# State-space scan with running sums loaded as rows, one input product for the context, and the last expert pair combined from SBUF

## What is computed

```python
a = (dt * A)                                   # per token and head, negative
a_cs = cumsum(a, in the chunk)                 # running sums
decay_to_end = exp(a_cs[..., -1:] - a_cs)
states = einsum('bclgn,bcgrl,bclgrp->bcgrpn', Bc, decay_to_end, xs * dt)
...
seg = a_cs[..., :, None] - a_cs[..., None, :]
Lm = exp(where(lower, seg, -inf))
cb = einsum('bclgn,bcsgn->bcgls', Cc, Bc)
y_diag = einsum('bcgls,bcgrls,bcsgrp->bclgrp', cb, Lm, x)
y_off = einsum('bclgn,bcgrpn,bcgrl->bclgrp', Cc, h_prev, exp(a_cs))
```

## Time and profile before

| | us |
|---|---|
| three runs | 3544.15, 3545.57, 3545.67 |
| median | 3545.57 |
| the profiled execution | 3550.36 |
| its span, first to last instruction | 3548.5 |

### The profile page before, as it was taken

One profiled execution on the slowest core, in us unless ns is written; L12 is line 12 of the kernel. 1 busy time (PEld: TensorE's weight loads), 2 busy tenths in 40 slices (PEclk: granted clock), 3 DMA queues, 4 the chain that ended last, 5 costly groups with the idle time before them and its releaser, 6 DMA issues. The chain is left out here.

```text
span 3548.5 us, 38000 instructions
## 1 busy us (share of the span) xinstructions
PE 3138.4 (88%) x15866; PEld 1657.4 (47%) x15866; DVE 1070.3 (30%) x2066; ACT 560.3 (16%) x1183; POOL 287.7 (8%) x270
## 2 busy tenths in 40 slices
PE   6997789998999999898999999997996789997984
PEld 5444644564554444653344434433545763544331
DVE  2233712554573301410111011103146453522112
ACT  2001510211452200100000000002012212301111
POOL 0003000002751000000000000000001200001101
PEclk9998999998899999899999999999998999997997
DMA  7721021110001222469999999997310012053996
GB/s 268 257 76 48 1 75 36 48 36 0 25 1 48 94 71 71 190 279 428 427 428 427 427 428 426 428 428 290 129 36 2 3 69 91 13 201 132 409 425 274
DMA packets 132081, 669.35 MB, mean 189 GB/s; under 512 B 17578, under 2 KB 45645, under 8 KB 98889
## 3 DMA queue, kind: packets, MB, share of 16 engines
q1 hardware_dynamic: 115385, 630.24, 44.0%
q10 hardware_dynamic: 11488, 28.31, 2.1%
q0 software_dynamic: 5040, 8.40, 0.7%
HBM read 672.15 MB, written 14.69 MB: 194 GB/s over the span
## 5 line engine op out<-in xcount | busy, mean ns | idle before, releaser
L2013 PE MATMUL ec_wide<-ec_ring,ec_xg 128*64 128x512 f32 x2048 | 459.8, 603 | 18.0 <-issue 13.8
L2013 PEld LDWEIGHTS ec_wide<-ec_ring,ec_xg 128*64 128x64 f32 x2048 | 147.9, 139 | 309.5 <-issue 305.4
L2047 PE MATMUL ec_acc<-ec_ring,ec_hidT 128*64 128x512 f32 x1024 | 233.6, 611 | 29.2 <-DMA ec_ring<-in_w_exp_down 28.4
L2172 DVE TENSOR_SCALAR ec_xg<-ec_piece,ordered 128x128 f32<-128x128 f32 x64 | 21.9, 404 | 570.8 <-PE ec_piece L2061 570.8
L2047 PEld LDWEIGHTS ec_acc<-ec_ring,ec_hidT 128*64 128x64 f32 x1024 | 81.9, 141 | 177.9 <-issue 177.8
L2061 PEld LDWEIGHTS ec_piece<-ec_sel,x 128*128 128x128 f32 x512 | 122.9, 336 | 8.6 <-issue 5.7
L2061 PE MATMUL ec_piece<-ec_sel,x 128*128 128x128 f32 x512 | 124.4, 405 | 2.8 <-DVE ec_sel L2154 2.8
L3700 PE MATMUL hm_gu<-hm_ring,hm_xg 128*64 128x512 f32 x432 | 115.7, 604 | 8.0 <-DMA hm_ring<-in_moe_w_gu 5.4
L2750 POOL TENSOR_TENSOR solve_T<-const_rw,solve_T 128x512 f32<-128x512 f32 x8 | 10.1, 1266 | 1311.7 <-DVE solve_T L2788 1311.7
L2136 ACT ACTIVATE ec_hidT<-ec_acc 128x512 f32<-128x512 f32 x32 | 17.4, 594 | 518.9 <-PE ec_acc L2036 518.9
L1151 PE MATMUL conv_main<-hT,conv_early 128*128 128x512 f32 x192 | 86.2, 604 | 2.9 <-DVE bcT L1233 2.9
(11 more groups left out here) (638 smaller groups left out, 5009.4 us busy)
## 6 DMA issues: line engine op xcount, KB each, us to landing
ec_ring<-in_w_exp_gate SPq DMA_DIRECT2D x64, 2048.0 KB, 17.7
ec_ring<-in_w_exp_up SPq DMA_DIRECT2D x64, 2048.0 KB, 27.0
ec_ring<-in_w_exp_down SPq DMA_DIRECT2D x64, 2048.0 KB, 19.5
hm_ring<-in_moe_w_gu SPq DMA_DIRECT2D x27, 2048.0 KB, 25.5
hm_ring<-in_moe_w_down SPq DMA_DIRECT2D x11, 2048.0 KB, 29.2
ahead_qkv<-in_w_in SPq DMA_DIRECT2D x10, 2048.0 KB, 9.7
hm_ring_late<-in_moe_w_down SPq DMA_DIRECT2D x5, 2048.0 KB, 25.2
u2T<-in_moe_w_gu SPq DMA_DIRECT2D x5, 2048.0 KB, 23.6
```

The source lines that it names most:

```text
L2013: last = pe.matmul(wide[half(e), b, :], xg[:, u % 2, j, half(e)], w[e][:, a, b * 512:(b + 1) * 512], start=(j == 0), stop=(j == KD - 1))
L2047: last = pe.matmul(acc[half(e), h, :], hidT[:, f, half(e)], w[e][:, r, h * 512:(h + 1) * 512], start=(f == 0), stop=(f == FT - 1))
```

## The change

In `steps_and_conv`: TensorE makes 8 more products behind the sums (running sums with the heads as rows), ScalarE copies them to `cumT`, copies the running sums with the tokens as rows into `a`, and stores `cumT` to DRAM (`cum_rows`); VectorE multiplies the decay to the end by `dt` once for all units. In `ssd_scan`: SP loads, per main unit, 1024 running sums into all 128 partitions (`crow`, 512 KB, 4 buffers, two of them in `hcT`); ScalarE forms max(0, own sum - row) in place and then its exponential with a minus; seg and seg_in are gone; `cb` has two buffers; xde is made from x directly, and context units have no xd. In `fine_experts`: the output of the last pair isn't stored; TensorE multiplies it by a one-hot matrix that carries the shares, VectorE adds the product, and the 8 loads no longer wait for the last pair.

```diff
@@ steps_and_conv, tensor, scalar, vector @@
+                for d, (bank, name) in enumerate(((prod, "upto"), (side[:, 1, :], "from"))):
+                    for t in range(LT):
+                        last = pe.matmul(bank[0:32, t * P:(t + 1) * P], a[:, t, d * 32:(d + 1) * 32], k.const(name), start=True, stop=True)
+                    last.then_inc(rows_summed, 1)
...
+            for d, bank in enumerate((prod, side[:, 1, :])):
+                act.wait_ge(rows_summed, d + 1)
+                act.activation(cumT[:, d, :], bank[0:32, :], ACT.Copy).then_inc(rows_taken, 1)
+            act.activation(a[:, :, :].rearrange("p t h -> p (t h)"), sums[0][:, 0:2 * N_SEG * 32], ACT.Copy).then_inc(exp_out, 1)
...
+            act.dma_start(cum_rows.rearrange("d t h l -> h d t l"), cumT.rearrange("h d (t l) -> h d t l", l=P)).then_inc(rows_stored, 16)
...
+                if i == R + 2:
+                    dve.wait_ge(decays_ready, 1)
+                    for d in range(2):
+                        m = slice(d * N_SEG, (d + 1) * N_SEG)
+                        dve.tensor_tensor(dec[:, m, 32:64], dt[:, :, d * 32:(d + 1) * 32], dec[:, m, 32:64], ALU.mult).then_inc(ended, 1)
@@ ssd_scan, sync @@
+            for m, n in enumerate(mains):
+                _, d, c, g = units[n]
+                unit = (d * LT + c) * SSD_G + g
+                if m >= CROWS:
+                    sp.wait_ge(exped, m - CROWS + 1)
+                sp.dma_start(crow[m % CROWS].rearrange("p h l -> p (h l)"), groups[unit:unit + 1, :].to_broadcast([P, HG * P])
+                             ).then_inc(crow_loaded[m % CROWS], 16)
+                if m == CROWS - 1:
+                    sp.wait_ge(inputs_ready, mains[0])
+                    then(sp)
@@ gpsimd @@
-                ins = pool.tensor_tensor(xd[:, n % 2].rearrange("p (h e) -> p h e", h=HG), x,
-                                         spread(dt[:, tile(units[n]), hs:hs + HG], 64), ALU.mult)
-                if n >= kept:
-                    ins.then_inc(inputs_ready, 1)
-                    return
-                link(ins)
...
+                if main:
+                    ins = pool.tensor_tensor(xd[:, n % 2].rearrange("p (h e) -> p h e", h=HG), x,
+                                             spread(dt[:, tile(units[n]), hs:hs + HG], 64), ALU.mult)
+                if n < kept:
+                    ins = pool.tensor_tensor(xde[:, n % 2].rearrange("p (h e) -> p h e", h=HG), x,
+                                             spread(dec[:, d * N_SEG + tile(units[n]), 32 + g * HG:32 + (g + 1) * HG], 64), ALU.mult)
+                ins.then_inc(inputs_ready, 1)
@@ tensor @@
-                for h in range(2):
-                    pe.matmul(seg[:, h, :], k.const("after" if d == 0 else "before"),
-                              seg_in[:, m % 2, 4 * h:4 * h + 4].rearrange("p h l -> p (h l)"), start=True, stop=True)
-                pe.matmul(cb[:, 0:P], bT[:, g, c * P:(c + 1) * P], cT[:, g, c * P:(c + 1) * P], start=True,
-                          stop=True).then_inc(seg_ready, 1)
+                if m >= 2:
+                    pe.wait_ge(masked, m - 1)
+                pe.matmul(cb[:, m % 2, 0:P], bT[:, g, c * P:(c + 1) * P], cT[:, g, c * P:(c + 1) * P], start=True,
+                          stop=True).then_inc(cb_ready, 1)
@@ scalar @@
+                for h in range(HG):
+                    row = crow[m % CROWS][:, h, :]
+                    ins = act.activation(row, row, ACT.Relu, scale=-1.0, bias=cum[:, d * N_SEG + c, g * HG + h:g * HG + h + 1])
+                ins.then_inc(falls_ready, 1)
...
+                act.activation(lx[:, m % 2], crow[m % CROWS], ACT.Exp, scale=-1.0).then_inc(exped, 1)
@@ fine_experts, gpsimd, tensor, scalar, vector @@
-            for b in range(2):
-                pool.wait_ge(y_stored[b], 16 * HM_PAIRS // 2)
-            pool.wait_ge(down_done, HM_PAIRS)
+            pool.wait_ge(y_stored[0], 16 * (HM_PAIRS // 2))
+            pool.wait_ge(y_stored[1], 16 * (HM_PAIRS // 2 - 1))
+            pool.wait_ge(down_done, HM_PAIRS - 1)
...
+                    for t in range(LT):
+                        last = pe.transpose(list_[:, t * P:(t + 1) * P], sel[:, u % 2, t, :], k.const("ident"))
+                    last.then_inc(weights_turned, 1)
...
+                for h in range(2):
+                    last = pe.matmul(combined[t % 2][:, h, :], sel[:, HM_PAIRS % 2, t, :], y[:, (HM_PAIRS - 1) % 2, h * 512:(h + 1) * 512],
+                                     start=True, stop=True)
+                last.then_inc(last_product, 1)
...
+                if u == HM_PAIRS - 1:
+                    act.wait_ge(weights_turned, 1)
+                    act.activation(sel[:, HM_PAIRS % 2, :, :].rearrange("p t n -> p (t n)"), list_[:, :], ACT.Copy).then_inc(weights_ready, 1)
...
+                    dve.scalar_tensor_tensor(out[:, t, :], back[:, 2 * t + i, :], earlier[:, i, t:t + 1], out[:, t, :], ALU.mult, ALU.add).then_inc(added, 1)
+                dve.wait_ge(last_product, t + 1)
+                dve.wait_ge(added, 3 * t + 2)
+                dve.tensor_tensor(out[:, t, :], out[:, t, :], combined[t % 2][:, :, :].rearrange("p b n -> p (b n)"), ALU.add).then_inc(added, 1)
```

More of the change, by code:

```diff
@@ L1076, in free, with steps_and_conv @@
         self.early.close()
-def steps_and_conv(k, hT, hcT, steps_in, weights, vec, taps, work, dt, a, dec, bcT, b_rows, bc_rows, xs, xsc):
+def steps_and_conv(k, hT, hcT, steps_in, weights, vec, taps, work, dt, a, decays, bcT, b_rows, bc_rows, xs, xsc):
     nc = k.nc
@@ L1796, in first_mixer @@
                     dec = tile(s1, "dec", [P, 2 * N_SEG, 96])
+                    cum_rows = nc.dram_tensor("ssd_cum_rows", [2, LT, SSD_H, P], F32, kind="Internal").ap()
                     bcT = tile(s1, "bcT", [P, 2 * SSD_G, L])
@@ L3782, in gathered_tokens, with last_weights @@
                                   scale_cols.unsqueeze(2).to_broadcast([P, KD, P]), ALU.mult).then_inc(xg_ready, 1)
+            def last_weights():
+                u = HM_PAIRS - 1
+                for e in range(2):
+                    link(dve.scalar_tensor_tensor(weight[:, e], first[:, :, :], float((2 * u + e) * SLOTS - 1), here[:, :, :], ALU.is_equal, ALU.mult))
+                    link(dve.tensor_tensor(weight[:, e, 0, :], weight[:, e, 0, :], weight[:, e, 1, :], ALU.add))
+                    dve.tensor_tensor(sel[:, u % 2, :, half(e)], sel[:, u % 2, :, half(e)],
+                                      weight[:, e, 0, :].unsqueeze(2).to_broadcast([P, LT, SLOTS]), ALU.mult).then_inc(weighted, 1)
+                link(dve.scalar_tensor_tensor(earlier[:, :, :], first[:, :, :], float(last_rows) - 1.5, here[:, :, :], ALU.is_lt, ALU.mult))
             one_hots(0)
@@ L3802, in _ @@
                     gathered_tokens(u + 1)
-            for n in range(BACK):
-                t, i = n // 2, n % 2
-                dve.wait_ge(fetched[n], 16)
-                if i:
-                    dve.wait_ge(added, n)
-                dve.scalar_tensor_tensor(out[:, t, :], back[:, n, :], here[:, i, t:t + 1], out[:, t, :], ALU.mult, ALU.add).then_inc(added, 1)
+                if u + 3 == HM_PAIRS:
+                    last_weights()
+            for t in range(LT):
+                for i in range(2):
+                    dve.wait_ge(fetched[2 * t + i], 16)
+                    if i:
+                        dve.wait_ge(added, 3 * t + i)
+                    dve.scalar_tensor_tensor(out[:, t, :], back[:, 2 * t + i, :], earlier[:, i, t:t + 1], out[:, t, :], ALU.mult, ALU.add).then_inc(added, 1)
+                dve.wait_ge(last_product, t + 1)
+                dve.wait_ge(added, 3 * t + 2)
+                dve.tensor_tensor(out[:, t, :], out[:, t, :], combined[t % 2][:, :, :].rearrange("p b n -> p (b n)"), ALU.add).then_inc(added, 1)
             link(dve.tensor_scalar(rank[:, :, :], rank[:, :, :], -float(SLOTS), None, ALU.add))
```

99 lines of the change are left out of this document (54 added, 45 removed).

## The result

| | before | changed |
|---|---|---|
| median, 20 runs each (us) | 3548.99 (3544.15 to 3554.21) | 3554.36 (3550.30 to 3558.81) |
| ratio, 95% interval | | 1.0014, 1.0008 to 1.0020 |
| span of the profiled execution (us) | 3548.5 | 3551.6 |
| TensorE, VectorE, ScalarE, GpSimd busy (us) | 3138.4, 1070.3, 560.3, 287.7 | 3132.7, 1082.4, 563.6, 264.3 |

The changed kernel is 0.14% slower, some 5 us (2.8 to 7.1), which is less than the 0.2% named as "no change"; with 20 runs each the interval leaves 1 out, so the small loss is real. Two large products a unit are gone from TensorE, yet its busy time fell by only 6 us: the work that is left there runs at a lower clock.

What follows compares the result with a forecast made beforehand. TensorE was taken to bound convolution and the first sixteen main units, GpSimd and VectorE next. Terms 1.8 - 2.6 - 0.5 - 3.4 + 1.7 - 5.0 - 2.1 + 12.8 = +2.7 on 3545.57 gave 3548.3 us; range 3531 to 3563.

Steps and rivals of the forecast that it cites:

- way into the main units: Between context and main units: a seg is lost, but cb, st, yo, yd run serially at low clock; -0.5 (-1.5 to +0.5).
- first sixteen, clock held: First sixteen main units at 2.4 GHz: unit falls from 5.45 to 5.24 us, -3.4 in all.
- last eight, clock held: Last eight main units at 2.4 GHz: unit falls from 5.93 to 5.1 us, -5.0 in all.
- clock falls, last sixteen and first sixteen: Main units: pauses without seg cause eight falls of 1.6 us, +12.8 (+5 to +21); none in the first sixteen.
- experts: End of experts: loads start 5.65 us earlier, eight adds, four PSUM adds and one 0.9 wait follow; -2.1 (-4 to +0.5).
- Only one runs at a time, and the one that came first goes first: Scan: any GpSimd instruction, mix and the late add into y exclude each other; early unit 5.24 us.
- the port isn't the next bound: Rival, main units: VectorE gets its operands first, early units come down to 4.5 us; 3522.9 in all, chance 0.08.
- some units reach 6.35. I take 6.2: Third eight main units: queueing gives 5.84, a delaying decay 6.35; 6.2 taken against 5.99, +1.7 (-1.2 to +2.9).
- I take none: First sixteen main units: no clock falls counted, as a fallen unit leaves about 7.4 us of gapless TensorE work; cost 0.
- a yd of 3.5: Sign against the forecast: yd of 3.5 us among the first sixteen main units would show the clock falling there.
- The rival on that side: Clock falls in the first sixteen too: half of sixteen units, 8 x 1.6 = +12.8 more, 3561.1; chance 0.13.
- Rows: Row loads and ScalarE work in the scan: cost nothing, loads being ahead; bound +10 once.

Runs made afterwards that it cites:

- filled_late: Changed kernel plus unused TensorE products ahead of yd, six in main units 16 to 23, eight in the last eight: 0.9955, 3534.55 us.
- scan_alone: Changed kernel with fine_experts as before (all 16 stores, 8 adds): ratio to before 1.0018.
- before_context: Kernel before plus unused products in its context units (18 ahead of the first state product, then three or five a unit): ratio 0.9976.
- two_unused: Changed kernel plus two unused 128-column products ahead of yd, only in the last eight main units: ratio to before 0.9994.
- psum_operands: Changed kernel with masked cb and off + yd written to PSUM, so no VectorE ring instruction has two SBUF operands: 0.9935, 3528.76 us.
- mask_alone: Changed kernel with only the masked cb put in PSUM; the late add into y stays in SBUF: ratio to before 0.9949.
- two_row_buffers: Changed kernel with two buffers for the rows of running sums in place of four: ratio to before 1.0096.

## Why the prediction was right, and where it was not

**The outcome.** No measurable change was the likeliest class, and 3554.36 lies in the range. The forecast was +2.7, measured +5.0 (2.8 to 7.1). Its terms:

| | predicted | measured |
|---|---|---|
| convolution | +1.8 | +1.95 |
| context | -2.6 | -2.6 |
| way into the main units | -0.5 | -1.5 |
| first sixteen, clock held | -3.4 | -2.3 |
| third eight, clock held | +1.7 | -1.8 |
| last eight, clock held | -5.0 | -4.2 |
| clock falls, last sixteen and first sixteen | +12.8, 0 | +14.3, +0.5 |
| behind the scan (z products start at 1.2 GHz) | 0 | +0.7 |
| experts | -2.1 | -1.4 |
| sum | +2.7 | +3.7 |

How the right column comes out: "clock held" is the period of undisturbed units, 16 x 5.32, 8 x 5.77 and, from filled_late, 7 x 5.19, less the stretch of before (87.4, 48.0, 40.5); what the stretches in the table of thirds have above that (85.6 - 85.1, 48.7 - 46.2, 48.1 - 36.3) is the clock. Convolution is the start of one tile to the next, 10.62 before and 12.57 in scan_alone and filled_late, where the same tile ran at the low clock. The changed kernel's own profile had the tile ahead of them at 2.4 GHz, 1.7 less; that is chance, since before and before_context, which are the same up to there, differ in it too (8.83 and 7.13). The two clock terms and the way into the main units are those of one trace: scan_alone and two_unused, the same in their first 24 main units, have 50.4 and 50.5 in the third eight where the changed kernel has 48.7, and 7.13 in place of 6.81 on the way in. The sum lies within the measured interval; other stages vary by more than its distance from 5.0.

**The mechanism was right.** "Only one runs at a time, and the one that came first goes first" gave 5.24 for the early unit and it is 5.32; psum_operands takes this order of queueing away, and the unit falls to 4.43; mask_alone does the same for the first sixteen with the mask's place alone. The rival "the port isn't the next bound" named 4.5 as the unit without it: right as a number, wrong as an event. The Trainium skill (SBUF — State Buffer, section "SBUF: two separate sides") gives this rule, the port pair locked for a whole VectorE instruction with two SBUF inputs, against a GpSimd instruction that reads SBUF; the trace agrees, mix 2.04 behind xde with them and 1.22 beside it without.

**Third eight: the step "some units reach 6.35. I take 6.2" failed.** The first layout of that step, 5.84, was right (5.77 measured). The alternation with 6.35 rested on the decay delaying state add, off and the first add; in the trace VectorE waits 1.03 for the decay and is through with off at 1024.8, when yd has just ended (xd, which waits for yd, starts at 1024.70), so the delay costs the first add next to nothing. The error of 3.5 us is the largest of the mechanical terms.

**The clock: right in sum, wrong in kind.** I priced eight falls of 1.6 us, each a single slow yd after a pause of 2.1 or more. What happened: two falls in the third eight from which TensorE came back, and a third at its end (2.5 us in all) that lasted, eight units at 1.2 GHz (11.8 us). The pause itself was no longer 2.1 there but 0.95, less than the 1.10 that "holds" in the earlier trace rows; I read that row as a rule on the length of a pause, when it only showed that a clock that is up stays up behind such pauses. two_unused shows the other half: once down, a pause of 0.95 in each unit kept it down in the changed kernel, and two unused products ahead of yd brought it back. What brought it back by itself in mask_alone is open. That my total was near is luck as to the parts.

**First sixteen: "I take none" was wrong in fact and right in cost.** The clock fell in them (window clock 0.92). The sign that the prediction named, a yd of 3.5, didn't show it, since the low stretches fell on st and yo (up to 2.04 and 1.91 us) and yd took 2.20 at most. But the fallen unit brings itself back without a pause, as the text said it would, and the whole cost 0.5 us, since the ring had 1.33 a unit to spare. The rival on that side, 12.8 for the same falls, failed by its price.

**Experts: the term was mis-sized.** Of -2.1, -1.4 came. The lead came out as foreseen (7.71 from the store that is waited for to the first add, before 7.79), and an add from PSUM takes 1.22 as assumed; in the profile of the changed kernel the wait between the first and second add was 1.69, not the 0.9 that I had taken. Over the ten kernels with the new end that wait is 1.1 on the mean, which is 0.2 of the 0.7; the other 0.5 is that the profile before, from which I reckoned, was a long one (26.3 for a stretch of 25.8 on the mean).

**Way into the main units.** -1.5, the end of the interval given: from the last context product to the first yd 6.81 in place of 8.26. Two segs stood there, 2.56 and 1.71; what they leave is partly taken back by st and yo of the first main unit, now 1.84 and 1.59 at the low clock in place of 0.86 each.

**Rows.** Nothing, as said; the cover is the lead of three units, and two_row_buffers gives its price.

## What to carry to other kernels

When work is taken off the engine that bounds a stage, read first what the pauses do to it: here TensorE gave back in clock what it had been relieved of, and filling the pauses with unused products was worth some four times the change's own loss. Before an order of instructions is tuned, look where operands lie: VectorE with two SBUF operands and GpSimd take turns, and a mask left in PSUM ended that at no cost. And a stage that runs at the low clock hides what its other engines could do, so a part of a change may look worthless until the clock is up.

## What the runs showed of the hardware that I had not expected

- A low clock can be stable at short pauses: 0.95 us in each 6.87, and yet 1.2 GHz from 1040 us to the end of the scan. Two unused products a unit (0.87 us at that clock) broke it. Stable is not fixed: in mask_alone it rose once, for one unit, behind pauses no shorter.
- In the context units a pause of 0.93 or more in 2.97 to 3.2 went with 1.2 GHz for 45 us in every kernel without unused products; with three such products a unit they ran at 2.4 GHz throughout, with pauses of 0.28, and in before_context with five, with pauses of 0.56 to 1.66.
- The decay on GpSimd, 1.04 alone, took 2.02 on account of a mix that had begun 0.92 before it; with one operand of mix in PSUM both overlapped at full speed, and writing the mask or the sum back into PSUM cost VectorE nothing (0.29 and 0.69, as into SBUF).
- The same two product groups behind the sums cost 1.95 us in the convolution in every kernel, but whether the tile ahead of them ran at the low clock (8.83 against 7.13) changed from one kernel to the next with no edit near it.
